# Norm sums with the ones held and the squares streamed, and a new order of rough scores and value products in latent attention

## The reference

```python
def rms_norm(x, g):
    xf = x.astype(jnp.float32)
    y = xf * lax.rsqrt(jnp.mean(xf * xf, axis=-1, keepdims=True) + EPS)
    return (y * g.astype(jnp.float32)).astype(x.dtype)
...
        hs = modulate(xs, g[0], ml[:, 0], ml[:, 1])          # rms_norm, then scale and shift
        if layer % 2 == 0: ... retention and neighbourhood attention
        else:              ... latent attention (mla_latent, mla_context)
        xs = gated_residual(xs, ys, g[1], ml[:, 2])          # x + gate * rms_norm(y)
        hs = modulate(xs, g[2], ml[:, 3], ml[:, 4])
        xs = gated_residual(xs, channel_mixer(hs, w_mlp_in[layer], w_mlp_out[layer]), g[3], ml[:, 5])
...
        s = jnp.concatenate([einsum(q, k) for q, k in zip(qs, ks)], axis=-1) * scale   # latent attention
        p = jax.nn.softmax(s, axis=-1)
        out = p @ v                                          # per head: 512 queries, 640 keys
```

## Time and profile before

| | |
|---|---|
| three runs | 1761.57, 1761.82, 1763.85 us; median 1761.82 |
| profiled execution | 1763.56 us, span 1761.8 us |
| PE | busy 1698.2 us (96%), 10934 matmuls |
| DVE, ACT, POOL | 1055.4 (60%), 730.7 (41%), 215.7 us (12%) |
| mean granted TensorE clock | 0.985 |
| chain that ended last | PE 83%, DVE 7%, issue 3%, ACT 3%, DMA 3% |

### The profile page before, as it was taken

One profiled execution on the slowest core, in us unless ns is written; L12 is line 12 of the kernel. 1 busy time (PEld: TensorE's weight loads), 2 busy tenths in 40 slices (PEclk: granted clock), 3 DMA queues, 4 the chain that ended last, 5 costly groups with the idle time before them and its releaser, 6 DMA issues.

```text
span 1761.8 us, 26947 instructions
## 1 busy us (share of the span) xinstructions
PE 1698.2 (96%) x10934; PEld 1516.7 (86%) x10934; DVE 1055.4 (60%) x1694; ACT 730.7 (41%) x1238; POOL 215.7 (12%) x204
## 2 busy tenths in 40 slices
PE   5999999899999999999999999999999999999997
PEld 2999864689999999999999973335999999999997
DVE  3778666945657777775574646667374653333345
ACT  3433245655653313213345745554465431231334
POOL 0000014422100000000220403433310000000011
PEclk8999999999999999999999989999999999999998
DMA  9454312031465456572321500002244722222231
GB/s 331 153 179 157 89 45 69 14 108 47 122 188 159 126 178 174 153 206 73 102 46 40 147 13 1 1 1 57 64 132 138 207 75 76 81 72 73 78 90 60
DMA packets 266796, 181.67 MB, mean 103 GB/s; under 512 B 26237, under 2 KB 239090, under 8 KB 265650
## 3 DMA queue, kind: packets, MB, share of 16 engines
q1 hardware_dynamic: 266674, 179.96, 34.9%
HBM read 173.75 MB, written 3.62 MB: 101 GB/s over the span
## 4 chain that ended last, share of the span: by engine, by line
PE 83%; DVE 7%; issue 3%; ACT 3%; DMA 3%; POOL 1%; SPq 0%; DVEq 0%; ACTq 0%; POOLq 0%
PE ps L820 21%; PE ps L822 21%; PE ps L821 21%; PE ps L1404 3%; PE ps L1414 1%; DMA ada_a<-in_w_ada 1%; DMA stage<-in_w_mlp_out 1%; DVE w_lo L571 1%; PE ps L999 1%; PE ps L1000 1%; PE ps L1001 1%; PE ps L876 1%; PE ps L1033 1%; PE ps L1015 1%; PE ps L1313 1%
## 5 line engine op out<-in xcount | busy, mean ns | idle before, releaser
L562 ACT ACTIVATE w_hi<-stage 128x1024 fp32r<-128x1024 f32 (+1 forms) x176 | 184.8, 1052 | 621.5 <-PE ps L822 502.0
L571 DVE TENSOR_TENSOR w_lo<-stage,w_hi 128x1024 fp32r<-128x1024 f32 (+1 forms) x176 | 218.2, 1241 | 294.6 <-ACT w_hi L562 294.5
L820 PE MATMUL ps<-hM_hi,w_lo 128*128 128x320 f32 x952 | 295.3, 310 | 0.0
L822 PE MATMUL ps<-hM_hi,w_hi 128*128 128x320 f32 x952 | 294.2, 309 | 0.0
L821 PE MATMUL ps<-hM_lo,w_hi 128*128 128x320 f32 x952 | 294.1, 309 | 0.0
L820 PE MATMUL ps<-h_hi,w_lo 128*128 128x320 f32 x824 | 256.0, 311 | 3.4 <-DVE h_lo L2497 2.6
L822 PE MATMUL ps<-h_hi,w_hi 128*128 128x320 f32 x824 | 254.6, 309 | 0.0
L821 PE MATMUL ps<-h_lo,w_hi 128*128 128x320 f32 x824 | 254.6, 309 | 0.0
L2722 POOL TENSOR_TENSOR rstd<-rstd,sq 128x320 f32<-128x320 f32 x73 | 76.5, 1056 | 972.4 <-ACT sq L1490 971.0
L820 PEld LDWEIGHTS ps<-hM_hi,w_lo 128*128 128x128 f32 x952 | 178.7, 188 | 3.4 <-issue 3.4
L821 PEld LDWEIGHTS ps<-hM_lo,w_hi 128*128 128x128 f32 x952 | 178.8, 188 | 0.0
(11 more groups left out here) (412 smaller groups left out, 3513.7 us busy)
## 6 DMA issues: line engine op xcount, KB each, us to landing
stage<-in_w_mlp_out SPq DMA_DIRECT2D x83, 512.0 KB, 3.9
stage<-in_w_mlp_in SPq DMA_DIRECT2D x80, 512.0 KB, 4.1
slab_mlp<-in_w_ada SPq DMA_DIRECT2D x28, 1024.0 KB, 5.2
stage<-in_w_in_ac SPq DMA_DIRECT2D x28, 512.0 KB, 3.9
slab_ac<-in_w_ada SPq DMA_DIRECT2D x12, 1024.0 KB, 6.1
ada_a<-in_w_ada SPq DMA_DIRECT2D x8, 1024.0 KB, 17.0
stage<-in_w_out_ac SPq DMA_DIRECT2D x8, 512.0 KB, 3.8
stage<-in_w_out_c SPq DMA_DIRECT2D x8, 512.0 KB, 3.8
```

Of the source, the lines that this page charges most:

```text
L562: nc.scalar.activation(hi_place(n)[:, 0:width], stage[:, n % STAGE, 0:width], ACT.Copy)\
L571: nc.vector.tensor_tensor(lo_place(n)[:, 0:width], stage[:, n % STAGE, 0:width], hi_place(n)[:, 0:width].bitcast(F32), ALU.subtract).then_ ...
L820: mm(out, lo[:, k], xh, start=j == 0, stop=False)
L822: last = mm(out, hi[:, k], xh, start=False, stop=j == k_tiles - 1)
```

## The change

In the norms, ones (128x128) are now loaded and the squares stream, 320 columns for each term. The result stands at once on all partitions, along the row; root and reciprocal are taken on 128x320, in PSUM, and `spread_root` is gone with its calls. In attention, the 128 context keys of a head's four rough scores go into one bank and are reduced by one instruction (`rough_past`, `past_peak`), joined to the others by a small minimum; the rough scores of 512 keys alternate between banks 0 and 7 from the sixteenth on; they are issued beside i = 0 to 5, 8 and 9 (the last two for the pair after the next), and the value products stand at i = 5 and 9 alone.

```diff
+ROUGH_AT = {0: (1, 2), 1: (1, 3), 2: (1, 4), 3: (1, 5), 4: (1, 6), 5: (1, 7), 8: (2, 0), 9: (2, 1)}
+ROUGH_BANK = [7 if a % 2 and a >= 15 else 0 for a in range(4 * NH_MLA)]
...
-                for b, tokens in enumerate(blocks(s)):
-                    mm(out[:, b:b + 1], rstd[:, tokens], ones[:, 0:1], start=b == 0, stop=False)
+                mm(out, ones[:], rstd[:, half(s)], start=True, stop=False)
                 for k in range(max(1, n - DIRECT[name] + 1), n):
                     pe.wait_ge(sq_done[s], at + k + 1)
-                    for b, tokens in enumerate(blocks(s)):
-                        last = mm(out[:, b:b + 1], sq[:, k % 2, tokens], ones[:, 0:1], start=False,
-                                  stop=b == 2 and k == n - 1)
+                    last = mm(out, ones[:], sq[:, k % 2, half(s)], start=False, stop=k == n - 1)
                 last.then_inc(sums_done[s], 1)
-            def spread_root(name, s):
...
-                f(rs[:, no % 2, 3 * s:3 * s + 3], sums_at(name, s), ACT.Sqrt, scale=1.0 / features, bias=eps[:])\
+                f(spread(name, s), sums_at(name, s), ACT.Sqrt, scale=1.0 / features, bias=eps[:])\
...
-                nc.vector.reciprocal(rs[:, no % 2, 3 * s:3 * s + 3], rs[:, no % 2, 3 * s:3 * s + 3])\
-                    .then_inc(rs_ready[s], 1)
+                nc.vector.reciprocal(spread(name, s), spread(name, s)).then_inc(rstd_done[s], 1)
...
+            def rough_past(p, e):
+                h = 2 * p + e
+                pe.wait_ge(hh_done, h + 1)
+                if h:
+                    pe.wait_ge(r_copy, h)
+                for b in range(4):
+                    last = mm(ps[:, 1, P * b:P * (b + 1)], q_hi[e][:, P * b:P * (b + 1)], k_hi[e][:, TL:T],
+                              start=True, stop=True)
+                last.then_inc(a_s, 1)
...
                 for i in range(10):
                     turned_scores(p, i)
-                    if p < MLA_PAIRS - 1 and i < 8:
-                        rough_scores(p + 1, i // 4, i % 4)
-                    if p < MLA_PAIRS - 1 and i in (5, 9):
-                        latent_rows(p + 1, i // 9)
-                    if i in (3, 5, 7, 9):
+                    if i in ROUGH_AT:
+                        ahead, j = ROUGH_AT[i]
+                        if p + ahead < MLA_PAIRS:
+                            rough_scores(p + ahead, j // 4, j % 4)
+                    if p < MLA_PAIRS - 1 and i in (1, 5):
+                        rough_past(p + 1, i // 5)
+                    if p < MLA_PAIRS - 1 and i in (3, 7):
+                        latent_rows(p + 1, i // 7)
+                    if p and i == 5:
+                        values(p - 1, 4)
+                        weight_sums(p - 1)
+                    if i in (5, 9):
+                        values(p, i // 2 - 2)
                         values(p, i // 2 - 1)
-                    if p and i == 1:
-                        values(p - 1, 4)
-                    if p and i == 2:
-                        weight_sums(p - 1)
...
-                    if p < MLA_PAIRS - 2 and i in (5, 9):
-                        rounded_head(p + 2, i // 9)
-                    if p < MLA_PAIRS - 1 and i in (6, 9):
-                        latent_row(p + 1, i // 9)
+                    if p < MLA_PAIRS - 1 and i in (3, 7):
+                        latent_row(p + 1, i // 7)
+                    if p < MLA_PAIRS - 2 and i in (4, 8):
+                        rounded_head(p + 2, i // 8)
...
-                    if p and i < 2:
-                        late_sums(p - 1, i)
-                    if p and 3 <= i < 7:
+                    if p and i in (0, 2, 3, 4):
+                        late_sums(p - 1, *{0: (0, 0), 2: (0, 1), 3: (1, 0), 4: (1, 1)}[i])
+                    if p and 6 <= i:
```

More of the change, by code:

```diff
@@ L383, in build @@
         peak = [w_lo[:, side[e], T:T + 104] for e in range(2)]
+        peak_past = [w_lo[:, side[e], T + 104:T + 112] for e in range(2)]
         peak_ctx, ident_r = w_lo[:, side[0], 752:864], w_lo[:, side[0], 896:1024]
@@ L500, in sums_at @@
         def sums_at(name, s):
-            return ps[:, 7 - s, 480:483]
+            return spread(name, s)
         def spread(name, s):
-            return ps[:, 7 - s if name == "ckv" else 4 + s, 0:HALF]
+            bank = {"ckv": 7 - s, "in0m": 7, "in1m": 7, "in1": 7 - 3 * s}.get(name, 4 + s)
+            return ps[:, bank, 0:HALF]
         def norm_place(name, s, k):
@@ L1309, in rough_scores @@
                 a = 8 * p + 4 * e + b
-                if a:
-                    pe.wait_ge(a_max, a)
-                q = q_hi[e][:, P * b:P * (b + 1)]
-                mm(ps[:, 0, :], q, k_hi[e][:, 0:TL], start=True, stop=True)
-                mm(ps[:, 1, 0:NP], q, k_hi[e][:, TL:T], start=True, stop=True).then_inc(a_s, 1)
+                before = [x for x in range(a) if ROUGH_BANK[x] == ROUGH_BANK[a]]
+                if before:
+                    pe.wait_ge(a_max, peak_count(before[-1]))
+                if ROUGH_BANK[a] == 7:
+                    pe.wait_ge(m_out, 2)
+                mm(ps[:, ROUGH_BANK[a], :], q_hi[e][:, P * b:P * (b + 1)], k_hi[e][:, 0:TL], start=True, stop=True)\
+                    .then_inc(a_s, 1)
+            def rough_past(p, e):
[7 more added lines that the diff above has]
+                last.then_inc(a_s, 1)
             for j in range(12):
@@ L1349, in latent_rows @@
             def latent_rows(p, e):
-                pe.wait_ge(a_max, 8 * p + 4 * e + 4)
+                pe.wait_ge(a_max, 6 * (2 * p + e) + 6)
                 pe.wait_ge(pe_rows, 1)
-                if p + e:
-                    pe.wait_ge(r_copy, 2 * p + e)
-                else:
-                    pe.wait_ge(vm_out, 12)
-                if p == 1 and e == 0:
-                    pe.wait_ge(m_out, 2)
                 for b in range(4):
                     c = 4 * e + b
-                    last = mm(ps[0:97, 7, P * b:P * (b + 1)], peak[p % 2][:, c:c + 97], ident_r, start=True, stop=True)
+                    last = mm(ps[0:97, 1, P * b:P * (b + 1)], peak[p % 2][:, c:c + 97], ident_r, start=True, stop=True)
                 last.then_inc(r_t, 1)
@@ L1429, in _ @@
             context_rows(1)
+            latent_rows(0, 0)
             rough_scores(0, 1, 1)
@@ L1992, in _ @@
             rounded_head(0, 1)
+            context_row(0)
+            context_row(1)
             latent_row(0, 0)
-            for g in range(CTX):
-                context_row(g)
+            context_row(2)
+            context_row(3)
             rounded_head(1, 0)
@@ L2661, in pair_scaled @@
                 dve.wait_ge(m_out, p + 3)
+            past_peak(0, 0)
             for j in range(4, 8):
                 latent_peak(0, j)
+            past_peak(0, 1)
+            for j in range(2):
+                latent_peak(1, j)
             for p in range(MLA_PAIRS):
-                for i in range(8):
-                    if p < MLA_PAIRS - 1:
-                        latent_peak(p + 1, i)
+                for i in range(10):
+                    if i in ROUGH_AT and p + ROUGH_AT[i][0] < MLA_PAIRS:
+                        latent_peak(p + ROUGH_AT[i][0], ROUGH_AT[i][1])
+                    if p < MLA_PAIRS - 1 and i in (1, 5):
+                        past_peak(p + 1, i // 5)
                     if p == 0 and i < 4:
@@ L2687, in _ @@
             for e in range(2):
-                late_sums(MLA_PAIRS - 1, e)
+                for which in range(2):
+                    late_sums(MLA_PAIRS - 1, e, which)
             dve.wait_ge(m_sum, MLA_PAIRS)
```

89 lines of the change are left out of this document (44 added, 45 removed).

## The result

The changed kernel takes 1738.73 us (median of 4 runs, 1737.35 to 1740.12) beside 1762.69 us of the kernel before on the same chip: ratio 0.9864, 95% interval 0.9847 to 0.9881. Forecast were 1737 and a range of 1728 to 1752. The profiled execution took 1740.12 us, its span is 1738.3.

What follows compares the result with a forecast made beforehand. PE, busy 96% of the span, was taken as the bound. Norms -15.0 and attention -10.0 took 25.0 from the profiled 1763.56, giving 1738.6; the median being 1.7 lower, 1737 us, range 1728 to 1752.

Steps and rivals of the forecast that it cites:

- Norms, -15.0: All 18 norm halves: 16.7 us saved on PE, corrected for late places, PE's waits and the clock, -15.0 us.
- The places on the path: Three places where the longer root and reciprocal delay PE: two second halves in `in_c` (+3.1) and the end (+1.9).
- +3.1: `in_c`, second halves of `y0m` and `in1`: late reciprocals delay the work behind, and the gain of both halves is lost.
- The clock, -3.0: Half-rate stretches at 889.2 and 957.4: replacing one-column sums by streams of 320 columns restores the clock, -3.0 us for both.
- the rule weighed there: Clock gate rule from the Trainium skill: activity lifts the throttle, idleness restores it; by idleness alone the 3.0 us stay.
- Early rough scores, +1.0: Before pair 0: two rough scores more stand there, +1.0 us.
- Pair 0, 0: Pair 0 of attention stays as it is: no change.
- Pairs 1 to 6, -9.6: Attention pairs 1 to 6: 18.8 us without waits, 1.9 under 20.67; 1.6 taken for each, -9.6 us.
- Last pair, -1.4: Last attention pair: four visits fewer -0.4, a value product filling PE's 2.00 us wait for DVE -1.0.
- The rest, -4: From the last weight sums to the end: the share of the norms' -15.0 for the 6 halves there.
- Rival 3: Norms where DVE is full: reciprocals block weight splits and PE waits; if all 18 do, 34 us, 1771; chance 0.04.
- Rivals 1, 2 and 4: Attention gives nothing (1747); norms give only their chains (1747); waits stay despite second bank; 0.14, 1 and 2 together 0.04.

Runs made afterwards that it cites:

- old_inc: Changed kernel with the old norm form (small sums, narrow root and reciprocal, spread) for the second halves of `y0m` and `in1` only: 1739.22 us.
- ckv_old: Changed kernel with the old norm form (one-column sums, spread) for both halves of the key latents' norm only: 1741.01 us.
- values4: Changed kernel with value products back at four visits of a pair, the previous pair's last product at its second score tile: 1740.57 us.
- bank0: Changed kernel with every rough score in bank 0, without the second bank: 1748.32 us.
- pool_late: Changed kernel with POOL's low part of a finished pair's output moved to the pair's end, ACT's high part to the seventh score tile: 1733.88 us.
- dve_moves: Changed kernel with two DVE moves: first context half before pair 1's early peaks, out1's weight splits before pair 6's inverses: 1735.62 us.

## Why the prediction came out right, point by point

The forecast was 1737 and 1738.7 came. What the norms save on PE and what the second bank does were seen rightly. That the sum is so close is partly luck: the clock gave nothing in sum where 3.0 us were taken, and the pairs gave 2.5 us more than forecast.

- **Norms, -15.0: -13.9 alone.** From the first norm sum to the end the trace of norms alone is 12.4 us shorter than before (1355.1 against 1367.5), with as much half rate up to the end of attention (20.5 against 20.4 us); the forecast without its clock term was -12.0. PE's part was nearly exact: 1.08 us for a y half (1.16 forecast), 88 records, reciprocals of 2.17. The places on the path: the end +1.3 (1.0 forecast for `gy`), the root 0.50 us where 0.43 was taken. In `in_c` the forecast was +3.1; from `y0m`'s second sum to `cq`'s first PE takes 34.7 us instead of 34.4, though 1.9 us of matmuls had gone: about +2.2; `old_inc` says that the place as a whole is worth 0.1. PE's wait at `in1`'s second sum came, but at the `rstd` term (1.7 us), one term ahead of the one named.
- **The clock, -3.0: right at its place, wrong in sum.** Both stretches are gone from this trace, but one of them comes and goes by itself, and the half rate comes back in the opening (+1.5 us with the norms alone), in pair 0 (+1.3 likewise) and behind the last pair (+1.0). From the first norm sum to there half rate lasts 23.9 us, before it lasted 20.4. A clock term taken from two stretches and summed as if the other stretches stayed was the weakest step of the prediction. That PE need not be idle for the fall, as the rows at 957 showed against the rule weighed there, `ckv_old` showed once more.
- **Early rough scores, +1.0: +1.6.** At 13.7 us of half rate each, the opening takes 32.8 us with the new order and 31.2 with the old.
- **Pair 0, 0: +0.7,** the clock again: +1.3 with instructions that did not change.
- **Pairs 1 to 6, -9.6: -12.1.** The sum of a pair without waits was 18.8 and the truth 17.88. The step that was off is that values and weight sums cost 1.01 us "also side by side". In pair 1 of the changed kernel the four behind i = 5 take 3.59 us from start to start and the two behind i = 9 take 1.87, 5.46 in all, where 6.1 and 0.2 for the visits were taken; the rest of the pair, 12.4 us, is what was summed (12.5). Each place fewer is worth 0.3 us (0.9 for three, `values4`), where 0.15 was taken. What DVE takes from it was put at 0.3 a pair; it was 1.16 in pairs 2 to 5, by a cause that the prediction did not have: POOL. The two errors offset each other, and that pairs of 18.8 to 19.3 us came is luck in part.
- **What the shorter reductions carry** is less than the sum for DVE implied: with one bank, they and the grouping give 1.7 us in pair 1 and 0.2 in pairs 2 to 5.
- **Last pair, -1.4: -0.7.** The wait went from 2.0 to 2.4 instead of to 1.0. The product more is in it, but one of DVE's last sums ran beside POOL's subtraction (1.84 us, from 1192.73); the splits ahead of them cost 0.4.
- **The rest, -4: -1.9.** 1.0 of the difference is the half-rate stretch that now stands behind the last pair: the kernels without it take 541.2 to 541.3 us there (`values4`, `bank0`, `pool_late`, `dve_moves`, norms alone), those with it 542.3 (the changed one, `old_inc`, `ckv_old`).
- **Rival 3** got 0.04 because PE was busy in one window of 25 us. That shows no slack. The run with three reciprocals shows that 4.3 us more at each norm turn the gain into a loss.
- **Rivals 1, 2 and 4** did not come: attention alone gave 10.2 us, norms alone 13.9.

## What to carry to other kernels

Where two engines hand one bank to and fro, a second bank can be worth more than a shorter operation on either side; here 8.1 of the 12.1 us that pairs 1 to 6 gained hung on it. Before regrouping an engine's work, look at which pair of the same loop is the fastest: its difference from the others named a cause (a POOL operation beside short two-input DVE operations) that was worth 4.9 us once that operation, and ACT's ahead of it, stood elsewhere. Before reading a stretch's time as the cost of its instructions, compare how long half rate lasted in it. And test slack by tripling an operation, not by looking at how busy its neighbour is.

## What the runs showed of the chip that was not expected

- A DVE minimum of 128x4 takes 0.16 us alone and 1.14 beside a POOL subtraction; an addition of 128x512 takes 0.69 alone, 1.45 beside an addition on POOL, 2.03 beside the subtraction of 128x640; reductions from PSUM stay at 0.68.
- A half-rate stretch follows the one-column matmuls of `ckv`'s sums with PE busy throughout, in three traces of three; 18 such records in a row elsewhere (`old_inc`) bring none.
- The length of half rate in the opening goes with that stretch 70 us earlier: 10.2 us with it and 13.7 without it in the old order, 6.8 with it and 10.2 or 13.7 without it in the new one. Each 3.4 us more make the opening 1.3 to 1.8 us longer.
- Four records of a product with 64 columns of the array (512 tokens, fp32) cost 1.01 us alone and 0.91 behind another of the kind.
